# Plain one-hots of the gate tables on ScalarE instead of VectorE, and merged semaphores

## The reference, cut to what matters

```
q = (t @ w_query).reshape(T, 8, 2, 128)
s = einsum('thpk,pnk->thpn', q, sub_keys)          # two scores per head over 128 keys
s_val, s_idx = top_k(s, 16)
cand = s_val[..., 0, :, None] + s_val[..., 1, None, :]
best, pos = top_k(cand.reshape(T, 8, 256), 16)     # 128 chosen experts (slots) for a token
expert = ...                                       # 128 * index of key 1 + index of key 2
gate = softmax(best)
out = sum over the slots of gelu(t . u_emb[expert]) * gate * v_emb[expert]
```

## Time and profile before

| | |
|---|---|
| median of 3 runs | 3456.78 us (3446.84 to 3457.04) |
| span of the profiled execution | 3458.3 us |
| TensorE busy | 3376.2 us, 98% |
| VectorE busy | 2361.7 us, 68% |
| ScalarE busy | 1012.7 us, 29% |
| GpSimd busy | 1805.8 us, 52% |

### The profile page before, as it was taken

The page is one execution under the profiler, slowest core; times in us unless marked ns, Lnnn a source line. Parts: engine busy times, 40 slices in busy tenths (PEclk is TensorE's granted clock), DMA queues, the critical chain, the costliest instruction groups (busy, mean ns, idle before and its releaser), DMA issues.

```text
span 3458.3 us, 44792 instructions
## 1 busy us (share of the span) xinstructions
PE 3376.2 (98%) x16931; PEld 2936.1 (85%) x16931; DVE 2361.7 (68%) x3848; ACT 1012.7 (29%) x1160; POOL 1805.8 (52%) x904
## 2 busy tenths in 40 slices
PE   6999999999999999999999999999999999999998
PEld 3688888766788889999999999999888888888886
DVE  2278887755514659994888888764667776767666
ACT  3332211143223232223222222223333323233233
POOL 1220000212544446676666666667777777778764
PEclk8999999999999999999999999999999999999999
DMA  8656642564424226777677777788988888888872
GB/s 337 265 186 205 216 168 94 191 245 175 194 96 152 90 105 248 265 278 275 257 314 302 281 282 299 305 314 313 377 327 329 317 325 328 316 326 324 321 277 97
DMA packets 184619, 874.72 MB, mean 253 GB/s; under 512 B 16621, under 2 KB 77501, under 8 KB 97844
## 3 DMA queue, kind: packets, MB, share of 16 engines
q1 hardware_dynamic: 122160, 525.38, 42.0%
q0 software_dynamic: 38688, 281.15, 20.1%
q10 hardware_dynamic: 23652, 66.69, 5.1%
HBM read 803.78 MB, written 69.32 MB: 252 GB/s over the span
## 4 chain that ended last, share of the span: by engine, by line
PE 88%; DVE 7%; DMA 1%; POOL 1%; issue 1%; ACT 1%; ACTq 0%; DVEq 0%; SPq 0%; POOLq 0%
PE bank L2080 82%; PE bank L2336 2%; PE bank L2452 1%; DMA ring<-in_w_mod 1%; PE bank L2310 1%; DVE b L1845 1%; PE bank L2088 1%; POOL low L769 1%; DVE rows_a L1784 1%; DVE b L1825 0%; DVE rows_c L1784 0%; PE bank L2436 0%; DVE tiny L1840 0%; DVE rows_b L1784 0%; DVE low L1403 0%
## 5 line engine op out<-in xcount | busy, mean ns | idle before, releaser
L811 POOL TENSOR_TENSOR split<-ring,split 128x1024 fp32r<-128x1024 f32 x544 | 1303.9, 2410 | 542.4 <-ACT split L1146 540.4
L2080 PE MATMUL bank<-h_hi,split 128*128 128x384 f32 (+1 forms) x4608 | 1221.8, 341 | 8.3 <-POOL split L811 7.0
L1146 ACT ACTIVATE split<-ring 128x1024 fp32r<-128x1024 f32 x544 | 577.8, 1063 | 1608.7 <-PE bank L2080 1588.3
L2080 PE MATMUL bank<-split,a_split 128*128 128x512 f32 x4608 | 1045.0, 389 | 0.1
L2080 PEld LDWEIGHTS bank<-split,a_split 128*128 128x128 f32 x4608 | 865.1, 188 | 179.8 <-POOL split L811 0.5
L2080 PEld LDWEIGHTS bank<-h_hi,split 128*128 128x128 f32 x4608 | 839.7, 188 | 29.7 <-POOL split L811 8.9
L2080 PE MATMUL bank<-h_lo,split 128*128 128x384 f32 (+1 forms) x2304 | 785.5, 341 | 0.0
L1962 DVE TENSOR_TENSOR acc<-acc,bank 128x512 f32<-128x512 f32 x372 | 251.5, 683 | 289.7 <-PE bank L2080 288.7
L2080 PEld LDWEIGHTS bank<-h_lo,split 128*128 128x128 f32 x2304 | 433.6, 188 | 9.5
L2080 PE MATMUL bank<-hT_hi,w_hi 128*128 128x512 f32 (+1 forms) x768 | 290.5, 378 | 8.5 <-DVE hT_lo L1408 4.4
L2080 PE MATMUL bank<-hT_lo,w_hi 128*128 128x512 f32 (+1 forms) x768 | 288.2, 375 | 0.0
(11 more groups left out here) (315 smaller groups left out, 3787.3 us busy)
## 6 DMA issues: line engine op xcount, KB each, us to landing
ring<-in_u_emb SPq DMA_DIRECT2D x128, 1024.0 KB
ring<-in_v_emb SPq DMA_DIRECT2D x128, 1024.0 KB
ring<-in_w_mod SPq DMA_DIRECT2D x48, 1024.0 KB
ring<-in_w_in SPq DMA_DIRECT2D x44, 1024.0 KB
ring<-in_w_mod SPq DMA_DIRECT2D x64, 512.0 KB, 4.7
neurons<-tiny ACTq DMA_DIRECT2D x128, 192.0 KB
gate_table<-b ACTq DMA_DIRECT2D x6, 4096.0 KB, 14.7
weigh<-neurons SPq DMA_DIRECT2D x32, 768.0 KB
```

Source lines behind the costliest of these rows:

```text
L811: nc.gpsimd.tensor_tensor(split[:, r % 2, 1, at].bitcast(F32R), ring[:, r % 4, :, :].rearrange("p k n -> p (k n)")[:, at], split[:, r % 2, ...
L1146: nc.scalar.activation(split[:, q % 2, 0, at].bitcast(F32R), ring[:, q, :, :].rearrange("p k n -> p (k n)")[:, at], ACT.Copy)\
L2080: last = mm(out_, left[a].bitcast(F32R), right[b].bitcast(F32R), start=start and n == 0, stop=stop and n == 2)
```

## The change: plain one-hots on ScalarE

The plain one-hots move to ScalarE, where a one-hot takes two steps: the absolute value of (position minus index), and then max(0, 1 minus that). The first step is one instruction for each of the four tokens of a group, the second is one instruction for all four. The index columns are stored with a negative sign for this (`scale=-1.0` in the copy at line 1285). The gate part stays on VectorE. ScalarE's 72 units are written out instead of being in a loop, and `onehot_rows` for the groups of unit n+1 stands behind both `next_hi` of unit n and ahead of the neuron store and the GELU of unit n. TensorE waits for one more semaphore, `rows_made`.

```diff
+            def onehot_rows(grp):
+                act.wait_ge(slotT_made, 2)
+                act.wait_ge(onehot_used, grp + 1)
+                rows = onehot[:, grp % 2, :, 0, :]
+                for s in range(4):
+                    last = nc.scalar.activation(rows[:, s, :].bitcast(F32R), iota, ACT.Abs,
+                                                bias=expT[:, 1, 4 * grp + s:4 * grp + s + 1])
+                last.then_inc(row_step, 1)
+                act.wait_ge(row_step, grp + 1)
+                nc.scalar.activation(rows.bitcast(F32R), rows, ACT.Relu, bias=one_col, scale=-1.0)\
+                    .then_inc(rows_made, 1)
...
-            with act.Fori(0, CHUNKS) as chunk:
-                for k in range(CHUNK_UNITS):
-                    neurons(chunk * CHUNK_UNITS + (PRE + k), k % 4)
+            for unit in range(PRE, PRE + CHUNKS * CHUNK_UNITS):
+                k, chunk = (unit - PRE) % CHUNK_UNITS, (unit - PRE) // CHUNK_UNITS
+                for h in range(2):
+                    next_hi(unit, unit % 4, h)
+                if unit + 1 < PRE + CHUNKS * CHUNK_UNITS:
+                    for _ in range(GROUPS_AT[(k + 1) % CHUNK_UNITS]):
+                        onehot_rows(group)
+                        group += 1
+                finish_neurons(unit, unit % 4)
...
                 for s in range(4):
                     tok = slice(4 * grp + s, 4 * grp + s + 1)
-                    nc.vector.tensor_scalar(onehot[:, grp % 2, s, 0, :].bitcast(F32R), iota_bank, expT[:, 1, tok],
-                                            None, ALU.is_equal)
                     last = nc.vector.scalar_tensor_tensor(
...
             def gate_group(count, buf):
                 pe.wait_ge(onehot_made, count)
+                pe.wait_ge(rows_made, count)
                 pe.wait_ge(gbank_free, count)
```

More of the change, by code:

```diff
@@ L345, in hybrid_layer @@
         spill_stored = sem("spill_stored")
-        ln_squared = sem("ln_squared")
-        ln_std_made = sem("ln_std_made")
+        ln_on_act = sem("ln_on_act")
         gate_nat = sem("gate_nat")
@@ L350, in hybrid_layer @@
         gate_spread = sem("gate_spread")
-        gate_turned = sem("gate_turned")
         qk_loaded = [sem(f"qk_loaded{h}") for h in range(HEADS)]
@@ L377, in hybrid_layer @@
         ln_step = sem("ln_step")
-        ln_rstd = sem("ln_rstd")
         ln_scaled = sem("ln_scaled")
@@ L432, in hybrid_layer @@
         rows_used = sem("rows_used")
-        soft_in = sem("soft_in")
+        soft_on_dve = sem("soft_on_dve")
         soft_exp = sem("soft_exp")
-        slots_made = sem("slots_made")
         slotT_full = sem("slotT_full")
@@ L439, in hybrid_layer @@
         onehot_made = sem("onehot_made")
+        row_step = sem("row_step")
+        rows_made = sem("rows_made")
         onehot_used = sem("onehot_used")
@@ L1028, in gate_steps @@
                     act.wait_ge(rows_loaded, 16 * 12)
-                    act.wait_ge(ln_scaled, 8)
+                    act.wait_ge(ln_scaled, 9)
                     nc.scalar.activation(gates_in[:, C:L], bank[0:GATES, 6, :], ACT.Identity, bias=gate_b)\
@@ L1049, in gate_steps @@
                                 last = nc.scalar.activation(dst[:, ::-1] if d else dst, grow[2 + kind][r, at], ACT.Copy)
-                    last.then_inc(gate_turned, 1)
-                    act.wait_ge(gate_turned, 1)
+                    last.then_inc(gate_act, 1)
+                    act.wait_ge(gate_act, 1)
                     nc.scalar.activation(grow[2], grow[1], ACT.Abs).then_inc(gate_act, 1)
-                    act.wait_ge(gate_act, 1)
+                    act.wait_ge(gate_act, 2)
                     nc.scalar.activation(grow[3], grow[2], ACT.Exp, scale=-1.0).then_inc(gate_act, 1)
-                    act.wait_ge(gate_act, 2)
+                    act.wait_ge(gate_act, 3)
                     nc.scalar.activation(grow[4], grow[3], ACT.Ln, bias=one_col[0:64, :]).then_inc(gate_act, 1)
@@ L1077, in _ @@
                         act.wait_ge(ln_step, 9)
-                        nc.scalar.activation(ln_sq, convT, ACT.Square).then_inc(ln_squared, 1)
+                        nc.scalar.activation(ln_sq, convT, ACT.Square).then_inc(ln_on_act, 1)
                     if n == 2 and q == 2:
                         act.wait_ge(pass_full, 2)
-                        nc.scalar.activation(ln_std, bank[:, 6, :], ACT.Sqrt, bias=eps_col).then_inc(ln_std_made, 1)
+                        nc.scalar.activation(ln_std, bank[:, 6, :], ACT.Sqrt, bias=eps_col).then_inc(ln_on_act, 1)
                     if n == 3 and q == 0:
-                        act.wait_ge(ln_scaled, 8)
+                        act.wait_ge(ln_scaled, 9)
                         for f in range(CTILES):
@@ L1263, in neurons, with finish_neurons @@
                     next_hi(unit, q, h)
+                finish_neurons(unit, q, store, wait)
+            def finish_neurons(unit, q, store=True, wait=True):
                 if store:
@@ L1278, in _ @@
                     neurons(i * 4 + q, q)
-            act.wait_ge(soft_in, 1)
+            act.wait_ge(soft_on_dve, 1)
             nc.scalar.activation(gate, gate, ACT.Exp).then_inc(soft_exp, 1)
@@ L1285, in _ @@
                     nc.scalar.activation(expT[:, q - 1, :] if q < 3 else gate_rest,
-                                         bank[:, 6 + (q - 1) % 2, 0:TD], ACT.Copy)\
+                                         bank[:, 6 + (q - 1) % 2, 0:TD], ACT.Copy, scale=-1.0 if q == 2 else 1.0)\
                         .then_inc(slotT_made, 1)
@@ L1290, in _ @@
             act.sem_inc(table_stored, 16)
-            with act.Fori(0, CHUNKS) as chunk:
-                for k in range(CHUNK_UNITS):
-                    neurons(chunk * CHUNK_UNITS + (PRE + k), k % 4)
-                act.wait_ge(gbank_free, chunk * 16 + (1 + 16))
-                act.dma_start(gate_dram[bass.ds(chunk, 1), :, :, :].rearrange("a p i t -> p (a i t)"),
-                              stage.rearrange("p i t -> p (i t)")).then_inc(table_stored, 16)
+            def onehot_rows(grp):
[9 more added lines that the diff above has]
+                    .then_inc(rows_made, 1)
+            group = 0
+            for _ in range(GROUPS_AT[0]):
+                onehot_rows(group)
[6 more added lines that the diff above has]
+                    for _ in range(GROUPS_AT[(k + 1) % CHUNK_UNITS]):
+                        onehot_rows(group)
+                        group += 1
+                finish_neurons(unit, unit % 4)
+                if k == CHUNK_UNITS - 1:
+                    act.wait_ge(gbank_free, 1 + 16 * (chunk + 1))
+                    act.dma_start(gate_dram[chunk, :, :, :].rearrange("p i t -> p (i t)"),
+                                  stage.rearrange("p i t -> p (i t)")).then_inc(table_stored, 16)
             def a_hi(s, group):
@@ L1534, in _ @@
                     .then_inc(ln_step, 1)
-            dve.wait_ge(ln_squared, 1)
+            dve.wait_ge(ln_on_act, 1)
             nc.vector.tensor_reduce(ln_square_sum, ln_sq.rearrange("p f t -> p t f"), AX.X, ALU.add)\
@@ L1539, in _ @@
                 sum_late(r)
-            dve.wait_ge(ln_std_made, 1)
-            nc.vector.reciprocal(ln_inv, ln_std).then_inc(ln_rstd, 1)
-            dve.wait_ge(ln_rstd, 1)
+            dve.wait_ge(ln_on_act, 2)
+            nc.vector.reciprocal(ln_inv, ln_std).then_inc(ln_scaled, 1)
+            dve.wait_ge(ln_scaled, 1)
             for f in range(CTILES):
@@ L1552, in _ @@
                 sum_late(r)
-            dve.wait_ge(gate_act, 3)
+            dve.wait_ge(gate_act, 4)
             nc.vector.scalar_tensor_tensor(grow[5], grow[1], 0.0, grow[4], ALU.min, ALU.subtract)\
@@ L1565, in _ @@
             nc.vector.tensor_tensor(grow[2], grow[3], grow[5], ALU.add).then_inc(gate_dve, 1)
-            dve.wait_ge(gate_act, 4)
+            dve.wait_ge(gate_act, 5)
             for d in range(2):
@@ L1874, in _ @@
             nc.vector.tensor_tensor(gate_g, best_g, best_g[:, :, 0:1].to_broadcast([P, LT * PH, TOPK]),
-                                    ALU.subtract).then_inc(soft_in, 1)
+                                    ALU.subtract).then_inc(soft_on_dve, 1)
             for n in range(dots_done[0], PRE - 7):
@@ L1883, in _ @@
             nc.vector.tensor_tensor(gate_g, gate_g, soft[:, 32:64].unsqueeze(2).to_broadcast([P, LT * PH, TOPK]),
-                                    ALU.mult).then_inc(slots_made, 1)
+                                    ALU.mult).then_inc(soft_on_dve, 1)
             for n in range(PRE - 7, PRE - 3):
@@ L2271, in _ @@
             pe.wait_ge(gate_split_made, 2)
-            pe.wait_ge(ln_std_made, 1)
+            pe.wait_ge(ln_on_act, 2)
             for k in range(KT):
@@ L2483, in _ @@
                     if q == 0:
-                        pe.wait_ge(slots_made, 1)
+                        pe.wait_ge(soft_on_dve, 2)
                         pe.wait_ge(score_copied, 4)
```

## The result

The changed kernel takes 3756.59 us (median of 5 runs, 3754.91 to 3759.37); the kernel before took 3449.33 us beside it (median of 5, 3446.84 to 3457.04). The ratio is 1.0883, with a 95% interval of 1.0867 to 1.0899: slower by 307 us. 3740 us was forecast, with a range of 3635 to 3800.

The account below looks back on a forecast made before the run. The prediction took TensorE's matrix products to bound the kernel, busy 98% of the span. Waits of 196 us plus 87 us lost by the clock made 283 us, which on 3456.8 us gave 3740 us, range 3635 to 3800.

Parts of the forecast that it names:

- The place: Unit border: rows queue behind ScalarE's second `next_hi`, which starts after TensorE ends the unit, so nothing hides the first group's.
- The wait: TensorE at 60 unit borders, waiting for the first gate group's rows: 3.26 us each, 196 us (162 to 234).
- The clock: TensorE's clock falls from 2.4 to 1.2 GHz behind the waits: 1.45 us a border, 87 us (0 to 102).
- Rival D: Something else behind the longer border: two clock falls in a row (3850 us) or a late GELU; chance 0.06.
- a late GELU: ScalarE's GELU, up to 4 us later behind the rows, is late for its bank; no separate size or chance.
- the relief, the loop and the semaphores: VectorE's 131.1 us less work, ScalarE's written-out loop and the merged semaphores: each worth 0.
- The second groups: Second gate group of a unit (36 of 96): rows ready before TensorE wants them, so they cost nothing.
- A: TensorE's clock doesn't fall behind the waits, each standing between 8 us of dense products: 3653 us; chance 0.12.
- B: ScalarE loads tables ahead of the rows and the GELU, 1.28 us each: 77 us more, 3817 us; chance 0.05.
- C: At the border, rows are ready before TensorE wants them and so hidden: not slower, 3457 us; chance 0.05.

Follow-up runs that it names:

- e1_between: Changed kernel with the rows of unit n+1 made between ScalarE's two `next_hi` of unit n: 3453.02 us, ratio 1.0002 to the kernel before.
- e3_filled: Changed kernel plus 17 unread TensorE products of 128x384 ahead of each unit's first gate group: 3671.63 us, ratio 1.0629 to the kernel before.
- e4_rest_alone: Changed kernel with plain one-hots back on VectorE, without `onehot_rows` and the wait for `rows_made`: 3452.39 us, ratio 0.9999 to the kernel before.
- e6_relief_alone: e4_rest_alone without VectorE's plain one-hots for all groups but the first two: 3454.56 us, ratio 1.0004 to the kernel before.
- e7_second_alone: Changed kernel with only each unit's second group (36 of 96) on ScalarE, first groups on VectorE: 3454.73 us, ratio 0.9999 to the kernel before.
- e5_longer: Changed kernel with three more absolute values of 128x128 on ScalarE ahead of each group's rows: 3833.99 us, ratio 1.1103 to the kernel before.

## Why the prediction was right

**The place, right.** "ScalarE's second `next_hi` of a unit begins when TensorE has already ended that unit": the changed kernel has 60 waits and no more, and moving the same instructions by one line of ScalarE's order (e1_between) takes all of them away.

**The wait, right in sum, off in its parts.** 3.26 us for a border were forecast and 3.28 measured from start to start, 197 us against 196. That it fits so well is in part luck. The absolute values were longer than taken: 386 ns each and 1.26 us for four, against 1.18. The second step took 722 ns against 700, and from its end to TensorE's first product there are 0.10 us against 0.04. On the other side the forecast had 0.12 in this sum for filling the array again, which doesn't lie between these starts; e3_filled shows about 0.08 us for a border in the gate group's own products. Two values were right: ScalarE starts 0.38 us behind the start of the unit's last product, which is about 0.2 behind the place where the group would follow, and the next instruction comes 0.96 us behind its copy (0.97 was taken). The Trainium skill's formula, page "ScalarE: Activation LUTs", section "What ACT_TABLE_LOAD costs", gives 387 and 707 ns for the two; the trace agrees within 15 ns, better than my nearest rows did.

**The clock, right as a mechanism, mis-sized as a term.** 1.45 us for a border were forecast, with an upper end of 1.7. Measured are 106 / 60 = 1.77 by the starts and 110.5 / 60 = 1.84 by the granted clock, so even the upper end was too low. I let some waits pass without a fall and took 3.4 us for the longest fall. Every wait brought one, and 8 falls were twice as long. 60 x 0.32 = 19 us, which is nearly all of the 20 us between the forecast sum of 283 and the 303 by the starts. The result lies only 17 us above the forecast because the sum was set on 3456.8, which is 2 to 3 us above the medians of the kernel before in the later runs. Rival D had this doubling, at every border; it came at 8. Its other branch, a late GELU, did not come: all of TensorE's waits in the stage are at line 2476.

**Nothing for the relief, the loop and the semaphores, right.** The loop and the semaphores stood alone in e4_rest_alone, the relief was added in e6_relief_alone, and both were within the measurement's error of the kernel before. The size of the relief was off, without a price: 131 us less on VectorE were forecast, 87 came. The forecast took 341 ns for each of 384 instructions, yet they overlap with their neighbours. In the kernel before the next instruction starts 0.26 us behind a plain one-hot, which makes 384 x 0.26 = 100 us; the rest of VectorE's work took some 13 us more than before.

**The second groups, right.** e7_second_alone shows them to be free in the late place.

**The rivals.** A (no fall of the clock) is ruled out by the 60 falls; what it would have given, 3653, is near what the filled kernel took, in which the falls are prevented. B (table loads): ScalarE's instructions in the stage are these four groups and no load, so relu and abs ran here without a load of their own beside the GELU. The Trainium skill, page "ScalarE: Activation LUTs", section "Table sets: the hidden batching unit", has relu and abs in every table set; the trace agrees, for relu too:

```profile
L1144 ACT ACTIVATE split<-ring 128x1024 fp32r<-128x1024 f32 x145 | 153.6, 1060 | 586.0 <-PE bank L2103 586.0
L1298 ACT ACTIVATE onehot<-iota,expT 128x128 fp32r<-128x128 f32 x384 | 121.2, 386 | 0.0
L1302 ACT ACTIVATE onehot<-onehot,one_col 128x512 fp32r<-128x512 f32 x96 | 69.3, 722 | 3.1
L1269 ACT ACTIVATE tiny<-bank 128x384 f32<-128x384 f32 x72 | 34.0, 472 | 0.0
```

C (the rows are early) is what e1_between builds; the changed kernel does not.

## What to carry to other kernels

An idle engine is not a free one: before work is moved to it, look at what releases the instruction that will stand ahead of it in the queue. Here that was the end of the very unit whose successor needed the work, so 3 us of work on an engine that was 71% idle cost 5 us at each of 60 borders; half a unit earlier in the same queue it cost nothing. And price a new TensorE wait as the wait plus what the clock loses behind it, which was half as much again.

## What the runs showed of the hardware

- The granted clock reacts to waits of 2 to 4 us in steps: behind 2.17 us it fell in 39 of 60 cases, at 3.11 and at 3.99 us in all, and the fall lasted 3.4 or 6.8 us, nothing between. Which of the two goes with the moment of the fall: all 38 long falls of the changed kernel and of e5_longer began 0.68 us or more before the wait was over, and all 82 short ones at most 0.57 us before its end or behind it.
- TensorE's idle time can be spent on products that nobody reads and the kernel gets faster by it (3757 to 3672 us), because they hold the clock. That mends a symptom; moving the work cost less.
